# Three edits to a two-layer hybrid diffusion backbone: the hyena's step order with two gate products ahead of each merge, the attention's squares ahead of the mix, and 64-slot experts in the first layer

## The reference

```python
pl = split(modulate(rmsnorm(x)) @ w_in)      # projections for all mixers and the gates gpre
ym = mlstm(...); ya = diff_attention(...); yh = hyena(...)
g_m, g_a, g_h = split(sigmoid(gpre + mb))
y = g_m * (ym @ wm) + g_a * (ya @ wa) + g_h * (yh @ wh)
x = x + g1 * (y @ wo)
# experts: 32 of width 512, the top 2 of one of 4 groups for each token
x = x + g2 * sum_over_two( w * (silu(h @ w1[e]) * (h @ w3[e])) @ w2[e] )
```

```python
u = short_conv(concat(hx0, hx1, hv)); x0, x1, v = split(u)
z = v * x1
z = bidir_longconv(z, hf, hb) + bias * z
return x0 * z
```

## Time and profile before

| | |
|---|---|
| median of 3 runs | 3427.74 us (3423.18 to 3431.49) |
| the profiled execution | 3434.79 us, its span 3433.0 us |
| TensorE matmul busy | 3074.6 us, 90% of the span |
| TensorE weight load busy | 2592.7 us, 76% |
| VectorE busy | 2041.8 us, 59% |
| ScalarE busy | 1552.1 us, 45% |
| DMA | 615.09 MB, mean 179 GB/s |

### The profile page before, as it was taken

One profiled execution on the slowest core, in us unless ns is written; L12 is line 12 of the kernel. 1 busy time (PEld: TensorE's weight loads), 2 busy tenths in 40 slices (PEclk: granted clock), 3 DMA queues, 4 the chain that ended last, 5 costly groups with the idle time before them and its releaser, 6 DMA issues. The chain is left out here.

```text
span 3433.0 us, 46648 instructions
## 1 busy us (share of the span) xinstructions
PE 3074.6 (90%) x16828; PEld 2592.7 (76%) x16828; DVE 2041.8 (59%) x2969; ACT 1552.1 (45%) x2186; POOL 0.2 (0%) x4
## 2 busy tenths in 40 slices
PE   8898889979998987999999978788879986999998
PEld 7676766657776775898898747776567885899997
DVE  2444745557455745666666555555465545888885
ACT  2321335442343234666666343234334444677774
POOL 0000000000000000000000000000000000000000
PEclk8999999989999988999999989899989997999999
DMA  5110511124221423999999302341052233999994
GB/s 197 72 51 12 221 59 37 43 92 149 72 74 67 179 106 126 345 338 341 341 335 345 134 37 111 120 159 68 31 208 99 86 123 122 403 423 424 423 421 173
DMA packets 75887, 615.09 MB, mean 179 GB/s; under 512 B 9662, under 2 KB 11648, under 8 KB 13184
## 3 DMA queue, kind: packets, MB, share of 16 engines
q1 hardware_dynamic: 75776, 613.64, 46.3%
HBM read 612.56 MB, written 1.05 MB: 179 GB/s over the span
## 5 line engine op out<-in xcount | busy, mean ns | idle before, releaser
L183 PE MATMUL ps<-rounded,rounded 128*128 128x256 f32 (+1 forms) x1904 | 662.4, 348 | 104.3 <-DVE rounded L174 82.6
L184 PE MATMUL ps<-rounded,rounded 128*128 128x256 f32 (+1 forms) x1904 | 650.2, 341 | 0.0
L185 PE MATMUL ps<-rounded,rounded 128*128 128x256 f32 (+1 forms) x1904 | 649.8, 341 | 0.0
L174 DVE TENSOR_TENSOR rounded<-low_arena,rounded 128x1024 fp32r<-128x1024 f32 (+3 forms) x302 | 360.2, 1228 | 286.4 <-ACT rounded L170 286.2
L183 PEld LDWEIGHTS ps<-rounded,rounded 128*128 128x128 f32 x1904 | 375.6, 197 | 150.8 <-DVE rounded L174 95.7
L159 PEld LDWEIGHTS ps<-low_arena,high_arena 128*128 128x128 f32 x4096 | 467.0, 192 | 7.4 <-issue 2.4
L159 PE MATMUL ps<-low_arena,high_arena 128*128 128x128 f32 x4096 | 467.7, 275 | 2.0 <-ACT low_arena L2394 1.3
L2416 DVE TENSOR_TENSOR rounded<-high_arena,rounded 128x1024 fp32r<-128x1024 f32 x256 | 313.2, 1225 | 185.1 <-ACT rounded L2376 164.5
L184 PEld LDWEIGHTS ps<-rounded,rounded 128*128 128x128 f32 x1904 | 375.8, 197 | 36.7 <-issue 0.5
L185 PEld LDWEIGHTS ps<-rounded,rounded 128*128 128x128 f32 x1904 | 374.3, 197 | 37.2
L170 ACT ACTIVATE rounded<-low_arena 128x1024 fp32r<-128x1024 f32 (+3 forms) x302 | 307.8, 1057 | 206.7 <-PE ps L185 131.1
(11 more groups left out here) (332 smaller groups left out, 3848.2 us busy)
## 6 DMA issues: line engine op xcount, KB each, us to landing
high_arena<-in_e_w SPq DMA_DIRECT2D x248, 1024.0 KB, 7.3
high_arena<-in_e_w SPq DMA_DIRECT2D x68, 2048.0 KB, 9.2
low_arena<-in_d_wm SPq DMA_DIRECT2D x48, 1024.0 KB, 4.8
high_arena<-in_d_modlater SPq DMA_DIRECT2D x40, 1024.0 KB, 6.9
low_arena<-in_d_wml SPq DMA_DIRECT2D x32, 1024.0 KB, 4.9
low_arena<-in_d_wh SPq DMA_DIRECT2D x16, 1536.0 KB, 6.6
low_arena<-in_d_wa SPq DMA_DIRECT2D x16, 1536.0 KB, 6.6
low_arena<-in_d_wo SPq DMA_DIRECT2D x8, 1024.0 KB, 4.8
```

Of the source, the lines that this page charges most:

```text
L174: return v.tensor_tensor(lo, raw, hi.bitcast(F32), ALU.subtract)
L183: pe.matmul(out, l_hi, r_hi, start=(k == 0), stop=False)
L184: pe.matmul(out, l_lo, r_hi, start=False, stop=False)
L185: last = pe.matmul(out, l_hi, r_lo, start=False, stop=(k == n - 1))
```

## The change

The slots, weights and products ahead of a merge: the gate and value halves of a merge's tiles get buffers of their own, each split by an instruction of its own. Two gate products (of units 0 and 1) are done at the end of the stage before, no longer one; ahead of merges 2 and 0 the value half of tile 0 is split there too. In the attention's tail the second gate product stands behind `o_sums(KC-1)`, in the mLSTM's behind `turn(M_HEADS-1)`, with the remainders of parts 1 and 2 behind VectorE's last `emit`.

The hyena: on TensorE the synthesis of a unit moves one step later, and `turn` and `analyse` move back in the step. ScalarE and VectorE interleave each convolution with one weight, and VectorE's output operations of unit u-1 come first in step u.

The attention: the squares of q and k come ahead of and behind the last copy, before the wait for the mix, and both roundings come behind the square of the mix's output.

The experts: S is 64 in both layers, the overflow slots are 128 (SO), and `n_over` is 15 in layer `l = 0` and 7 in layer `l = 1` (7 and 7 before). The overflow turn waits for each of its three DMAs by itself and frees their places one by one. Layer `l = 0` runs the loop of layer `l = 1`, but with 4 buffers for split granules in place of 8: granules 4 to 7 of expert e are split in step e (`OWN`), 0 and 1 of e+1 behind them (`PRE`), 2 and 3 after the gate (`MID`).

```diff
 def gate_products(pe, K, l, branch, ahead, s, ks):
-    out = K.ps[:, gate_bank(branch, 0), 0:ns * SEQ]
+    out = K.ps[:, gate_bank(branch, s), 0:ns * SEQ]
...
@@ stage_hyena, TensorE @@
-            def step(u, s, more=True, first=False):
-                if more:
-                    project(u + 1, 1 - s, 0, None if first else u - 1)
+            def step(u, s, first=False):
+                project(u + 1, 1 - s, 0, None if first else u - 1)
+                if not first:
+                    synthesise(u - 1)
+                project(u + 1, 1 - s, 1, u)
                 turn(u, s)
...
+                project(u + 1, 1 - s, 2, u)
                 analyse(u)
...
-                synthesise(u)
...
+            gate_products(pe, K, l, 2, ahead, 0, range(KC))
+            synthesise(KC - 2)
+            turn(KC - 1, 1)
+            analyse(KC - 1)
+            pe.wait_ge(convolved, KC * 3)
+            gate_products(pe, K, l, 2, ahead, 1, range(KC))
+            synthesise(KC - 1)
...
@@ stage_hyena, ScalarE @@
+            def step(u, s, first=False, weights=True):
+                if not first:
+                    descale(u - 1)
+                for j in range(3):
+                    if j == 2:
+                        copy_z(u)
+                    centre(u + 1, 1 - s, j)
+                    if weights:
+                        weight(u + 2, s, j)
...
+            round_ahead(act, K, 2, ahead, 0)
+            descale(KC - 2)
+            round_ahead(act, K, 2, ahead, 1)
+            copy_z(KC - 1)
...
@@ stage_hyena, VectorE @@
+            def step(u, s, first=False, weights=True):
...
+                    output(ch, u - 1, 1 - s)
+                for j in range(3):
+                    convolve(ch, u + 1, 1 - s, j)
+                    if weights:
+                        weight(u + 2, s, j)
...
+                mix(ch, u, s)
...
@@ stage_merge, TensorE @@
+            pe.wait_ge(ahead.done, 2)
+            pe.sem_inc(projected, 1)
+            unit(0, 0, gated_ahead=True)
+            unit(1, 1, gated_ahead=True)
+            unit(2, 0)
...
@@ stage_attention, TensorE @@
             o_sums(KC - 1)
+            pe.wait_ge(v_copied, KC)
+            gate_products(pe, K, l, 1, ahead, 1, range(KC))
...
@@ stage_attention, ScalarE @@
+                if more:
+                    square(u + 1, 0)
                 copy(u, nq - 1)
+                if more:
+                    square(u + 1, 1)
+                act.wait_ge(mixed, u + 1)
+                act.activation(osq[:, t0:], K.ps[:, 7, t0:], ACT.Square).then_inc(o_squared, 1)
                 if more and then:
                     weights(u + 2, s, 1, q_projected)
-                act.wait_ge(mixed, u + 1)
-                act.activation(osq[:, t0:], K.ps[:, 7, t0:], ACT.Square).then_inc(o_squared, 1)
-                if more:
-                    squares(u + 1)
-                    if then:
-                        weights(u + 2, s, 2, k_projected)
+                    weights(u + 2, s, 2, k_projected)
...
@@ stage_mlstm, TensorE @@
             turn(M_HEADS - 1)
+            pe.wait_ge(unit_out, 2 * LAST)
+            gate_products(pe, K, l, 0, ahead, 1, range(KC))
...
@@ stage_moe @@
-    S = SLOT if ns == 2 else SLOT // 2
-    n_over = (A - 1) // S
+    S = SLOT // 2
+    SO = SLOT
+    n_over = (A - 1) // (S + 1)
...
-                        sp.wait_ge(o_down, b)
-                        for dst, src in expert_tiles(K, l, e, 1):
-                            sp.dma_start(dst, src).then_inc(o_in, 16)
+                        for (dst, src), used, landed in zip(expert_tiles(K, l, e, 1), (o_half, o_up, o_down), (o_in1, o_in3, o_in2)):
+                            sp.wait_ge(used, b)
+                            sp.dma_start(dst, src).then_inc(landed, 16)
...
+            homes = [152 + 8 * q for q in range(4)] + ([52, 60, 88, 96] if ns == 1 else [])
+            NB = len(homes)
+            PRE = range(EARLY // 2) if ns == 2 else range(EARLY)
+            MID, POST = (range(2, 4), range(0)) if ns == 2 else (range(EARLY, EARLY + 1), range(EARLY + 1, GR))
+            OWN = range(NB, GR)
...
+                        act.wait_ge(w_used, e * GR + (i + 1 - NB))
+                    act.activation(w_hi[i % NB], pair_of(i), ACT.Copy).then_inc(w_rounded, 1)
...
+                    for i in OWN:
+                        rest(e, i)
+                    if more:
+                        for i in PRE:
+                            rest(e + 1, i)
```

793 lines of the change are left out of this document (344 added, 449 removed).

## The result

The changed kernel takes 3387.0 us (median of 4 runs, 3376.29 to 3388.70), the kernel before 3429.6 beside it (4 runs, 3423.18 to 3433.45). The ratio is 0.9872, with a 95% interval of 0.9849 to 0.9894: faster by 1.3%. The forecast was 3365, so it is 22 too low, inside its range. The profiled execution took 3385.9 against 3434.8 before: 48.9 of the 63 us that the sum gave.

The account below looks back on a forecast made before the run. Expert loops were taken as bound by TensorE's matmul count, hyenas as waiting for VectorE. Terms -92 + 86 - 24 - 19 - 7 - 7 = -63 on 3434.8 gave 3371.8, less 7.05: 3364.7 us, range 3335 to 3410.

Parts of the forecast that it names:

- Expert loop: First layer's expert loop: the period falls from 18.56 to 15.6 us, gaining 92 us over 31 periods.
- (a): Rival, first layer's expert loop: granule pitch stays 1.35, 19 us less gain, 3384 us in all; chance 0.14.
- (b): Rival, first layer's expert loop: the four buffers suffice wholly, 19 us more gain, 3346 in all; chance 0.12.
- (d): Rival, first layer's expert loop: the four-buffer ring sets the whole loop, which gains nothing; slower, 3457 us; chance 0.08.
- walk of the four buffers: First layer's `raise_`: granules 4 to 7 made while it runs, the last ready at 6.9 against 6.3, 0.6 us late.
- Overflow: First layer's overflow block: three turns entered, 12 skipped, 95.2 us less 9.7 before, so +86; bounds +79 and +97.
- (e): Rival, overflow: the router on the chip counts otherwise and more blocks are entered, 24.3 us each, 3389 for one; chance 0.02.
- (c): Rival, first layer's overflow: code is fetched at each leap, 12 x 3.0 = 36 us more, 3401 in all; chance 0.07.
- Hyena: Hyena stages of both layers: reordering removes TensorE's waits for z and the half clock; -24 us first layer, -19 second.
- the ring: Second layer's hyena: VectorE's chain of work takes 13.4 us a step, 0.8 over the matmuls, a new wait of 5 us.
- Gate products: Merges and the tails ahead: products moved ahead, less new waits at unit 2; sum -7 us, bounds -16 and +6.
- Squares: Attention: squares moved before the mix start the rotation 0.8 us a head sooner in the first layer; -7 us in all.

Follow-up runs that it names:

- e4: Changed kernel with the second gate product back in the merge, made by unit 1, its weights still split ahead: 3368.1 us, ratio 0.9808 to before.
- e1: Changed kernel with ScalarE rounding the next q weights ahead of the square of the head's output in the attention: 3375.9 us, ratio 0.9832 to before.
- e6: Changed kernel with unit 0's output and tile 2's remainders ahead of modulation in merges, and tile 2 loaded ahead of modulation's tiles: 3366.5 us, ratio 0.9805.
- e9: Changed kernel with overflow turns 64 slots wide instead of 128: 3435.5 us, ratio 1.0004 to before.
- e2: Changed kernel with the squares of q and k back behind the output's square and q's rounding ahead of it: 3386.4 us, ratio 0.9861 to before.
- e8: Changed kernel with the expert stage of before the change in both layers: 3403.0 us, ratio 0.9908 to before.
- e12: Changed kernel plus q's rounding first, one gate product ahead, tile 2 loaded first, modulation in its old place, one test over later overflow turns: 3352.3 us, ratio 0.9766.

## Why the prediction was right or wrong

**The base.** The forecast took the profiled time of 3434.8 and 7.05 off it, since the median of three runs stood that much lower. That median didn't repeat: the kernel before gave medians of 3434.9, 3435.1, 3433.7 and 3433.3 in four later sets of 7, 7, 15 and 9 runs. And the changed kernel's profiled run is 1.1 under its median. These 8 us of the 22 are no mechanism. The other 14 are: gate products 13 over their term and squares 3, less 5 that hyenas and experts brought beyond theirs, and 2 elsewhere.

**Expert loop: right.** Forecast 15.6 a period, measured 15.57. Rivals (a), pitch of 1.35, (b), four buffers suffice, and (d), the ring sets the loop, are out: they would have shown 16.2, 14.97 and over 17.6. The walk of the four buffers (0.6 late) is borne out by the 0.61 in the last three granules.

**Overflow: right within 2.3, its terms less so.** Three turns were entered, and (e) is out. The first load made TensorE wait 11.47 where 9.3 was taken, half clock and turns together took 76.2 for 75.4, and what lies behind the last matmul 11.78, to be set against 10.5 for the skips and half a leap. The 9.7 subtracted for the kernel before stands in no row; its whole gap was 15.8. Rival (c) took 3.0 for each of 12 leaps; the trace of the changed kernel has 0.73 a skip and none over 1 us. The Trainium skill, Runtime: NRT & Kernel Launch, section Instruction fetch mechanics, says that a taken branch out of the pages held makes the engine fetch. The traces agree for one leap of a block in four places (3.36, 3.75, 3.73, 3.59 us), and only for the first of them: in each, a 16 KB transfer of the instruction queue starts 1.0 to 1.3 us after the leap begins and ends inside it. Whether a block has it changes between kernels with the same source in that place. The changed kernel has none, so the 1.5 that I took for it wasn't paid. The whole stage gained 7 more than forecast: 2.3 here, 1.9 in the first `raise_` and 2.2 behind the last transposes, two edges that "31 periods" left out.

**Hyena: right in the first layer** (-24.5 for -24, though the terms as written add up to -23.4). In the second -16.0 for -19: the ring takes 14.0 and not 13.4. VectorE's own work in it is 10.3, as taken (10.4). But it idles 2.80 over `synthesise` and the descale and 0.88 for the next centre, 3.7 where I had 3.0.

**Gate products: the step that failed.** The forecast had the new waits at unit 2 nearly at their size (4.57, 3.72 and 4.07 for 3.7, 3.0 and 4.2) and let a merge give back the difference between product and wait. It did not: the merges of the first layer changed by -3.0, +0.3 and -1.7 where -5, -2.6 and -4.6 were taken. The term that stood at nothing is the half clock behind the new wait, 1.7 us in merge 1. Counted over the whole stage (TensorE's busy time times what the granted clock lacks to 1), the lower clock costs the three merges 2.8, 2.3 and 1.9 us before and 3.5, 4.1 and 4.4 after. Ahead of the barriers, the one of the attention comes 3.1 later behind the last head's output sums, as forecast, and the one of the mLSTM 8.2 later behind the last head's transposes (13.1 for 4.9), where 6.6 was taken. The gate product there, behind a wait of 2.36, starts at half clock and takes 7.14 for 5.6. I had paid for half clock in the hyenas (7.5 and 7.0 there) and forgotten it here. e4 shows the size: 15 us less without the second product, some 13 if the attention's stretch at a lower clock is left out, where my own walk had made it 2 to 5. Around the first merges it is neutral.

**Squares: the other step that failed.** Forecast -7, found -3.8 (2.8 and 1.0 from the first rotation to the last). The step was "the rotation started at 637.90 because of the projections ahead of it": the earlier trace rows end the normed k at 637.02, but the rotation also waits for the output's root, which ended at 636.84 + 0.63 = 637.47, and I didn't look at it. So 0.4 a head was to be had at most, and 0.23 came. "A little over 1 in each last head" was right (1.4 and 1.0). The rounding put behind the output's square takes 0.95 of the same chain; e1 gives it back, 0.94 a head in both layers.

**The rest**, +2.1 over norm, out and the second layer's experts, is in the main the second layer's norm with its +2.7. It has the same 132 matmuls behind the same waits, and a lower clock. The rows of that stage, of the kernel before, of the changed kernel and of e6, whose norm has the changed kernel's source:

```profile
1998.90:2062.30 63.40, 44.31 (x132) 23.31 (x132) 32.14 (x52) 35.53 (x60) 0.00 (x0) 0.85 0.13 50
1966.90:2032.90 66.00, 46.97 (x132) 24.18 (x132) 32.27 (x52) 35.69 (x60) 0.00 (x0) 0.81 0.12 48
1953.10:2016.40 63.30, 44.29 (x132) 23.30 (x132) 32.14 (x52) 35.55 (x60) 0.00 (x0) 0.85 0.13 50
```

So it isn't the edit: with the clock back at 0.85 the stage takes 63.3 again. What moves the clock is open.

## What to carry to other kernels

When work is moved ahead of a barrier, count what the next stage can do with the time: here the first wait that came sooner took most of the gain, and the half clock behind it took more. Read who releases such a wait in the trace, and which semaphores an instruction waits for besides the one you move. In a chain through one engine (here ScalarE's from square to root) a rounding of 0.95 us put into it cost its whole length in each head, and one line out of it was worth more than the edit that was meant to help. Before a difference of 2 us in a stage is given a cause, look at the granted clock of both kernels in that stage, and at a kernel with the same source there.

## What the runs showed of the hardware

- In e9, over a block of float32 matmuls of 64 columns with a weight load each, the granted clock stayed at 0.50 (1.2 GHz) for 130 us; with 128 columns it was 0.62 in the first 9 us of the block and 0.97 behind them. Half the columns cost 1.7 to 1.8 times as much per turn (42.6 against 25.5 and 23.8 us, gate included).
- Behind the wait of 3.72 us in merge 1 TensorE lost 1.7 us to the lower clock. It isn't always so: e1 has the same wait with 3.65 us and full clock behind it (the row below). The gate product behind the wait of 2.36 us ahead of merge 0 takes 7.14 us in the changed kernel, with the granted clock at 0.50 for its first 3 us, and behind 2.35 us in e2 it takes 5.7 at 1.00.

```profile
733.00:741.00 8.00, 7.78 (x34) 6.48 (x35) 7.90 (x13) 0.69 (x1) 0.00 (x0) 1.00 0.68 262
```

- Stretches at half clock also come and go in code that no run had changed. One mLSTM head takes 62.6 or 64.3 us, another 42.3 or 44.0, always 1.7 apart. Two stretches of e1, then the same two of the changed kernel:

```profile
952.00:1016.00 64.00, 60.83 (x304) 50.74 (x303) 33.19 (x58) 24.72 (x45) 0.00 (x0) 0.97 0.19 65
1016.00:1060.00 44.00, 39.56 (x210) 33.03 (x209) 20.66 (x45) 15.44 (x33) 0.00 (x0) 0.96 0.08 26
```

```profile
952.00:1016.00 64.00, 60.83 (x312) 50.99 (x311) 33.46 (x59) 26.08 (x46) 0.00 (x0) 1.00 0.19 66
1016.00:1060.00 44.00, 39.56 (x217) 33.24 (x216) 23.20 (x47) 15.44 (x32) 0.00 (x0) 1.00 0.07 25
```

  In e1 this hides 6.9 of its 13.8 us in the span: its mLSTM stages are 4.2 and 2.7 longer than the changed kernel's.
- The first leap over a skipped turn took TensorE 3.4 to 3.8 us in four of the 27 blocks with skipped turns that were traced (3.36 before, 3.75 and 3.73 in e8, 3.59 in e12), with a 16 KB transfer of instructions inside it each time, and 0.2 in the others.
